# Prompt delta rule: projections as three passes of high and low parts, tokens split once, outputs kept in memory, the turns of k and v moved

## The reference

```python
proj = h @ w_in                                   # q_a, k_a, v_a, z_a: 8 heads x 128 columns each
q, k, v = silu(causal_conv(concat(q_a, k_a, v_a)))  # 4 taps
q = l2norm(q) * DK ** -0.5;  k = l2norm(k)
...
# chunked form of S_t = a_t S_{t-1} (I - b_t k_t k_t^T) + b_t k_t v_t^T,  o_t = S_t^T q_t
L = A + eye;  sol = triangular_solve(L, [v * beta, kb * exp(gc)])
def chunk_step(S, ...):
    v_new = u_n - w_n @ S
    o_n = q_n @ S + qk_n @ v_new
    S = S * ge + k_n.T @ v_new
...
o_a = rmsnorm(o_a, gdn_norm) * silu(z_a)
merged = sigmoid(gate_a) * (o_a @ w_br_gdn) + sigmoid(gate_b) * (o_b @ w_br_swa)
```

## Time and profile before

| | us |
|---|---|
| median of 3 runs | 3023.04 (3020.31 to 3026.46) |
| the profiled execution | 3019.03 |
| its span in the profile | 3017.4 |
| TensorE busy | 2488.4 (82%), 12055 records |
| VectorE busy | 1534.6 (51%) |
| ScalarE busy | 1060.1 (35%) |
| GpSimd busy | 390.5 (13%) |
| mean granted TensorE clock | 0.895 |

### The profile page before, as it was taken

One profiled execution on the slowest core, in us unless ns is written; L12 is line 12 of the kernel. 1 busy time (PEld: TensorE's weight loads), 2 busy tenths in 40 slices (PEclk: granted clock), 3 DMA queues, 4 the chain that ended last, 5 costly groups with the idle time before them and its releaser, 6 DMA issues. The chain is left out here.

```text
span 3017.4 us, 34539 instructions
## 1 busy us (share of the span) xinstructions
PE 2488.4 (82%) x12055; PEld 1842.5 (61%) x12056; DVE 1534.6 (51%) x2016; ACT 1060.1 (35%) x1517; POOL 390.5 (13%) x434
## 2 busy tenths in 40 slices
PE   4789999999995756789986989888937999999940
PEld 2367666776674633644445989883426888888720
DVE  2155455545544312124446464633346888888805
ACT  3123323322331100023333333321206777777702
POOL 1012012101201120012222000000022111111003
PEclk7899999999997757589997999999968999999965
DMA  7411111111101023031105544444246999999625
GB/s 287 169 38 37 37 30 52 36 37 30 52 5 49 19 83 129 1 84 42 42 1 195 148 125 145 127 141 151 78 176 261 401 405 406 405 403 403 258 104 188
DMA packets 313391, 436.14 MB, mean 145 GB/s; under 512 B 56354, under 2 KB 254514, under 8 KB 293539
## 3 DMA queue, kind: packets, MB, share of 16 engines
q1 hardware_dynamic: 289164, 370.93, 34.9%
q0 software_dynamic: 11168, 39.12, 3.5%
q10 hardware_dynamic: 13000, 25.30, 2.2%
HBM read 384.40 MB, written 52.94 MB: 145 GB/s over the span
## 5 line engine op out<-in xcount | busy, mean ns | idle before, releaser
L2417 DVE TENSOR_TENSOR ex_w_r<-ex_w,ex_wh 128x2048 fp32r<-128x2048 f32 x192 | 433.2, 2284 | 59.7 <-ACT ex_wh L2359 59.6
L2359 ACT ACTIVATE ex_wh<-ex_w 128x2048 fp32r<-128x2048 f32 x192 | 367.7, 1917 | 130.6 <-PEq L2066 43.0
L828 PE MATMUL gd_ps<-hT,gd_w 128*128 128x352 f32 x768 | 252.3, 483 | 8.1 <-DMA gd_w<-in_w_in_dram 7.4
L1779 PE MATMUL mg_psum<-mg_xl,mg_wh 128*128 128x352 f32 x768 | 251.4, 327 | 0.0
L828 PEld LDWEIGHTS gd_ps<-hT,gd_w 128*128 128x128 f32 x768 | 151.6, 202 | 91.0 <-issue 13.8
L1839 DVE TENSOR_TENSOR mg_w_r<-mg_w,mg_wh 128x1024 fp32r<-128x1024 f32 x96 | 133.9, 1399 | 118.8 <-ACT mg_wh L1792 118.4
L1792 ACT ACTIVATE mg_wh<-mg_w 128x1024 fp32r<-128x1024 f32 x96 | 101.3, 1056 | 183.2 <-DVE mg_out L1866 120.1
L1951 PE MATMUL op_mix<-op_w,op_mT 128*128 128x512 f32 x288 | 130.6, 613 | 25.0 <-DMA op_w<-in_w_out_dram 25.0
L1779 PEld LDWEIGHTS mg_psum<-mg_xl,mg_wh 128*128 128x128 f32 x768 | 147.7, 192 | 0.0
L1779 PE MATMUL mg_psum<-hT_r,mg_wh 128*128 128x352 f32 x384 | 126.2, 329 | 18.4 <-DVE mg_w_r L1839 18.4
L1475 PE MATMUL wp_proj_psum<-hT,wp_wq 128*128 128x512 f32 x256 | 116.2, 608 | 14.0 <-DMA wp_wk<-in_w_in_dram 8.8
(11 more groups left out here) (576 smaller groups left out, 5195.0 us busy)
## 6 DMA issues: line engine op xcount, KB each, us to landing
ex_w<-in_w_gate_dram SPq DMA_DIRECT2D x64, 1024.0 KB, 8.0
ex_w<-in_w_up_dram SPq DMA_DIRECT2D x64, 1024.0 KB, 7.4
ex_w<-in_w_down_dram SPq DMA_DIRECT2D x64, 1024.0 KB, 8.6
ada_w<-in_w_ada_dram SPq DMA_DIRECT2D x24, 1024.0 KB, 16.0
mg_w<-in_w_in_dram SPq DMA_DIRECT2D x48, 512.0 KB, 3.5
gd_w<-in_w_in_dram SPq DMA_DIRECT2D x32, 512.0 KB, 4.2
expert_out_scratch<-ex_y ACTq DMA_DIRECT2D x32, 512.0 KB, 7.7
mg_w<-in_w_br_gdn_dram SPq DMA_DIRECT2D x24, 512.0 KB, 3.9
```

What stands on the lines that cost most here:

```text
L828: last = nc.tensor.matmul(dst, w[t][:, n, :], c.hT[:, n, at], start=(n == 0), stop=(n == KD - 1))
L1779: last = nc.tensor.matmul(pm[b][q][:, 0:R], a, x, start=(m == 0 and v == 0), stop=(m == KD - 1 and v == 2))
L2359: nc.scalar.activation(wh[at][:], wl[b][u][:], ACT.Copy).then_inc(w_high, 1)
L2417: nc.vector.tensor_tensor(wl_r[b][u][:], wl[b][u][:], wh[at][:].bitcast(F32), ALU.subtract).then_inc(w_low, 1)
```

## The change

- All projections of `delta_prompt` become three passes of fp32r: `wh` (high part of the weight, two buffers for four weights), `w_r` (its low part, in place of the weight), `hh` and `hl` (the two parts of the tokens; the low part lies in place of `hT`).
- For each weight and head, ACT casts the high part (`high`) and VectorE subtracts it (`low`). Both are put at fixed places in the streams.
- Before the first head the tokens are split in eight steps on ACT and VectorE, with the q projection of head 0 following step by step. Behind the last head GpSimd adds the halves up into `hT` again.
- The outputs go to `qd` and from there to memory (`c.oa_s`); `conv_outputs` loads them back into `c.oaT`, which is now allocated behind `delta_prompt`. `nwT` shares a buffer with `k2`.
- TensorE does the first third of the next q ahead of the turn of k, and the turn of v within level 4 instead of ahead of it.

```diff
@@ sync: body, behind the store of the state
+                    for g in range(2):
+                        sp.wait_ge(o_done, i * 2 + g + 1)
+                        sp.dma_start(c.oa_s[bass.ds(i, 1), :, g * C4:(g + 1) * C4].rearrange("a p t -> (a p) t"), qd[g][:]).then_inc(oa_stored, 16)
...
                 sp.wait_ge(stored, 16 * H)
+                sp.wait_ge(oa_stored, 32 * H)
@@ gpsimd: behind the heads
+                for n in range(KD):
+                    pool.wait_ge(v_proj, 3 * H)
+                    nc.gpsimd.tensor_tensor(c.hT[:, n, :], hl[:, n, :].bitcast(F32), hh[:, n, :].bitcast(F32), ALU.add).then_inc(joined, 1)
@@ scalar
+                def high(t, j):
+                    act.wait_ge(w_loaded[t], j * 16 + 16)
...
+                    nc.scalar.activation(half_of(t)[:], w[t][:], ACT.Copy).then_inc(w_high, 1)
@@ scalar: body
                         nc.scalar.activation(DT[g][:], E[g][:], ACT.Exp).then_inc(dt, 1)
+                    if nxt:
+                        high(0, i + 1)
                     for t in range(2):
...
                     evac(2, 2, i)
+                    if nxt:
+                        high(1, i + 1)
+                        evac(0, 0, i + 1)
                     for g in range(2):
                         act.wait_ge(turned, i * 2 + g + 1)
                         nc.scalar.activation(kt[g][:], X[g][0][:], ACT.Copy).then_inc(kts, 1)
-                    if nxt:
-                        evac(0, 0, i + 1)
...
+                        high(3, i + 1)
...
+                    if nxt:
+                        high(2, i + 1)
                     for g in range(2):
                         act.wait_ge(wt, i * 2 + g + 1)
                         nc.scalar.activation(nwT[g][:], pp[g][:], ACT.Copy, scale=-1.0).then_inc(nw, 1)
@@ scalar: before the heads
+                high(0, 0)
+                for n in range(KD):
+                    nc.scalar.activation(hh[:, n, :], c.hT[:, n, :], ACT.Copy).then_inc(h_high, 1)
+                high(1, 0)
@@ vector
+                def low(t, j):
+                    dve.wait_ge(w_high, split_count(t, j))
+                    nc.vector.tensor_tensor(w_r[t][:], w[t][:], half_of(t)[:].bitcast(F32), ALU.subtract).then_inc(w_low, 1)
@@ vector: body; low(0) stands before the norms, low(3) behind level 5, low(2) in the last chunk
                     dve.wait_ge(normed, i * 4 + 4)
+                    dve.wait_ge(oa_stored, i * 32)
...
                     conv(2, i, 0, CONV)
+                    if nxt:
+                        low(1, i + 1)
                     solve(i)
...
-                        nc.vector.scalar_tensor_tensor(c.oaT[:, bass.ds(i, 1), at].rearrange("p a t -> p (a t)"), E[g][:], 0.5, DT[g][:], ALU.mult, ALU.mult).then_inc(o_done, 1)
+                        nc.vector.scalar_tensor_tensor(qd[g][:], E[g][:], 0.5, DT[g][:], ALU.mult, ALU.mult).then_inc(o_done, 1)
@@ vector: before the heads
+                low(0, 0)
+                for n in range(KD):
+                    dve.wait_ge(h_high, n + 1)
+                    nc.vector.tensor_tensor(hl[:, n, :], c.hT[:, n, :], hh[:, n, :].bitcast(F32), ALU.subtract).then_inc(h_low, 1)
+                low(1, 0)
...
-                for t in range(2):
-                    conv(t, 0, 0, CONV)
+                low(3, 0)
+                conv(0, 0, 0, CONV)
+                low(2, 0)
+                conv(1, 0, 0, CONV)
@@ tensor
+                def passes(t, n, at):
+                    return ((half_of(t)[:, n, :], hh[:, n, at]), (half_of(t)[:, n, :], hl[:, n, at]), (w_r[t][:, n, :], hh[:, n, at]))
...
-                        last = nc.tensor.matmul(dst, w[t][:, n, :], c.hT[:, n, at], start=(n == 0), stop=(n == KD - 1))
+                        for v, (a, b) in enumerate(passes(t, n, at)):
+                            last = nc.tensor.matmul(dst, a, b, start=(n == 0 and v == 0), stop=(n == KD - 1 and v == 2))
@@ tensor: body
+                    if nxt:
+                        pe.wait_ge(v_evac, i * 3 + 3)
+                        for half in range(2):
+                            project(0, 0, half, i + 1)
                     for g in range(2):
                         pe.wait_ge(ats, i * 8 + g * 4 + 4)
                         turn(X[g][0], y[1], g).then_inc(turned, 1)
                     if nxt:
-                        pe.wait_ge(v_evac, i * 3 + 3)
-                        for u in range(3):
+                        for m in range(1, 4):
                             for half in range(2):
-                                project(0, u, half, i + 1)
-                    pe.wait_ge(v_silu, i + 1)
-                    pe.wait_ge(capped, i * 8 + 8)
-                    for g in range(2):
-                        turn(pp[g], y[2], g).then_inc(vturned, 1)
...
+                                project(m // 3, m % 3, half, i + 1)
@@ tensor: levels, between the two products of level 4
-                        if nxt and l > 4:
+                        if l == 4:
+                            pe.wait_ge(v_silu, i + 1)
+                            pe.wait_ge(capped, i * 8 + 8)
+                            for g in range(2):
+                                turn(pp[g], y[2], g).then_inc(vturned, 1)
+                        elif nxt:
                             project(1, l - 4, 0, i + 1)
@@ conv_outputs, sync
                 sp.dma_start(c.wkv[:], kmajor(w_in[0])[:, :, CKB:CKB + 2 * KVH * DH]).then_inc(c.kv_loaded, 16)
+                sp.dma_start(c.oaT[:, :, 0:T], c.oa_s.rearrange("h p t -> p h t")).then_inc(oa_loaded, 16)
...
                 sp.wait_ge(stored, 32)
+                sp.wait_ge(oa_loaded, 16)
```

More of the change, by code:

```diff
@@ L444, in delta_prompt @@
         k = Kit(nc, ctx)
-        w = [k.sb(f"gd_w{t}", [P, KD, P]) for t in range(4)]
+        w, w_r = zip(*(k.sb_reused(f"gd_w{t}", [P, KD, P]) for t in range(4)))
+        wh = [k.sb(f"gd_wh{n}", [P, KD, P], F32R) for n in range(2)]
+        hh, hl = k.sb("gd_hh", [P, KD, TA], F32R), c.hT_r
         pre = k.sb("gd_pre", [P, 3, CONV - 1 + T])
@@ L456, in delta_prompt @@
         grp = lambda n: [k.sb(f"gd_{n}{g}", [P, C4]) for g in range(2)]
-        E, DT, qd, qkm, AT, Y, YT, T1, k2, kdt, vt, nwT = (grp(n) for n in (
-            "E", "DT", "qd", "qkm", "AT", "Y", "YT", "T1", "k2", "kdt", "vt", "nwT"))
+        E, DT, qd, qkm, AT, Y, YT, T1, k2, kdt, vt = (grp(n) for n in (
+            "E", "DT", "qd", "qkm", "AT", "Y", "YT", "T1", "k2", "kdt", "vt"))
+        nwT = k2
         am = [[k.sb(f"gd_am{g}{b}", [P, C4]) for b in range(2)] for g in range(2)]
@@ L469, in delta_prompt @@
         gn_loaded = sem("gd_gn_loaded")
+        w_high, w_low, h_high, h_low, oa_stored, joined = (sem("gd_" + n) for n in ("w_high", "w_low", "h_high", "h_low", "oa_stored", "h_joined"))
+        RANK = (0, 1, 3, 2)
         halo, staged, qk_taps, qk_proj, qk_evac, v_proj, v_evac, z_proj, z_evac = (sem("gd_" + n) for n in (
@@ L593, in evac @@
                     src = pp[u % 2] if t == 3 else (pps, pv, pps)[u]
+                    if t == 0 and u == 2 and isinstance(j, int) and j == 0:
+                        src = pp[0]
                     if t == 3 and u == 0:
@@ L777, in body @@
                             nc.vector.tensor_copy(YT[g][:], X[g][1][:]).then_inc(yts, 1)
-                        if nxt and l == 4:
-                            conv(0, i + 1, 2, CONV)
+                        if nxt:
+                            if l == 4:
+                                conv(0, i + 1, 2, CONV)
+                            else:
+                                low(3, i + 1)
                     for g in range(2):
@@ L796, in body @@
                                 silu_qk(1, i + 1)
+                            if ch == CONV + 3:
+                                low(2, i + 1)
                     for g in range(2):
@@ L840, in z_unit @@
                         pe.wait_ge(z_evac, j * 3 + 1)
-                    last = nc.tensor.matmul(pp[u % 2][:, 0:C3], w[3][:, k_, :], c.hT[:, k_, u * C3:(u + 1) * C3], start=(k_ == 0), stop=(k_ == KD - 1))
+                    for v, (a, b) in enumerate(passes(3, k_, slice(u * C3, (u + 1) * C3))):
+                        last = nc.tensor.matmul(pp[u % 2][:, 0:C3], a, b, start=(k_ == 0 and v == 0), stop=(k_ == KD - 1 and v == 2))
                     if k_ == KD - 1:
@@ L971, in body @@
                         nc.tensor.matmul(X[g][1][:], c.ones[:], T1[g][:], start=True, stop=True).then_inc(o_sum, 1)
-                for t in (0, 1, 3):
+                pe.wait_ge(w_low, 1)
+                for n in range(KD):
+                    pe.wait_ge(h_low, n + 1)
+                    for u in range(3):
+                        for v, (a, b) in enumerate(passes(0, n, slice(u * C3, (u + 1) * C3))):
+                            last = nc.tensor.matmul((pps, pv, pp[0])[u][:, 0:C3], a, b, start=(n == 0 and v == 0), stop=(n == KD - 1 and v == 2))
+                        if n == KD - 1:
+                            last.then_inc(qk_proj, 1)
```

(1 more changed line is left out.)

37 lines of the change are left out of this document (25 added, 12 removed).

## The result

The changed kernel takes 3031.89 us (median of 20 runs, 3026.16 to 3037.59) against 3023.94 for the kernel before in the same comparison: a ratio of 1.0024, 95% interval 1.0015 to 1.0032. The prediction said 3033, slower. TensorE is busy for less time, 2419.7 us where it was 2488.4, and the kernel takes longer.

What follows compares the result with a forecast made beforehand. A chain over ScalarE, TensorE, VectorE and DMA up to level 4, not TensorE, bounds each head; +2 - 16 + 14.6 + 2.5 + 7 = +10.1 us on the median of 3023.04 gives 3033, range 3012 to 3050.

Steps and rivals of the forecast that it cites:

- start: Before the first head: subtractions and casts ahead of convolutions and tanh, z's last unit waiting longer; +2 us, 0 to +4.
- seven periods: Seven heads with a next one: period 100.55 us against a mean of 102.81, 2.26 less each; -16 us together.
- last head: Last head: three v units give 3.0 us, turn of v costs 2.0, GpSimd's additions cost 15.6; together +14.6.
- joins: Last head: GpSimd's eight additions of token halves each let one VectorE solve step pass; +15.6 us, 0 if steps slip between.
- last output store: Behind the heads: the block's end waits for the last output store and its issue; +2.5 us, 0 to 5.
- reload in `conv_outputs`: Behind the heads: 4 MB of outputs loaded back behind wkv make the next stage start 7 us later, 4 to 11.
- low(1): Between convolution and solve on VectorE: subtraction for k's weights lies on the chain to level 4; +1.2 us, 0 to 2.2.
- Rival (A): Heads: TensorE sets the period, so its saved 84 us come out; change of -58 us, 2965 us; chance 7%.
- The scores: Ahead of level 4: the scores start 2.1 us earlier, after the waiting cast of q's weights; bounds 3.0 and 0.
- Rival (C): Ahead of the scores: q's weights land 2 us or more later than forecast, scores gain nothing; 3048 us; chance 16%.
- The half clock and the turn of v: From level 4 on: first products at 1.2 GHz after idle time, v's transposition behind them; +4.1 us per head.
- Rival (B): Last head: GpSimd's additions of the token halves cost nothing; -5.5 us, 3017.5 us; chance 17%.

Runs made afterwards that it cites:

- the old order: The changed kernel with the turns of k and v and q's first third back where they were, projections in three passes: 3018.02 us, ratio 0.9973.
- the two runs on the joins: Changed kernel with GpSimd's last-head additions waiting for the solve's end: 3016.49 us, ratio 0.9969; changed kernel with each addition cut in two: 3033.82 us, one run.
- the order alone: The kernel before with only the turns of k and v and q's first third moved, projections still full fp32: 3042.71 us, ratio 1.0055.

## Why the prediction was right

Its forecast case came, by its own terms, measured from the start of the last decay sums and the stages around them:

| term | forecast | measured |
|---|---|---|
| start | +2 | -0.1 (158.82 against 158.92; see below) |
| seven periods | -16 | -18.1 (701.84 against 719.90) |
| last head | +14.6 | +15.8: 14.5 up to level 4 (joins +17.1, the rest -2.6), 1.3 from there to the outputs |
| last output store | +2.5 | +2.3 |
| reload in `conv_outputs` | +7 | +6.1 |
| sum | +10.1 | +6.1 |

- **The bound.** The two parts of a head, 50.35 and 50.2 us, came out at 50.39 and 49.81. That the chain sets the first is shown by the runs with low(1) and with the solve moved. Rival (A) falls: over heads 1 to 6 TensorE's busy time fell by 9.9 us a head (96.5 to 86.6), of which 7.3 became idle time (6.3 to 13.6) and 2.6 shortened the head. The prediction read the floor's distance, 2.6 us, from head 1, whose first part of 53.84 us was an unusual one before; in the other heads with a next one it was 52.64 to 52.68. The sum used 51.25 and the mean period and is not touched by this.
- **The scores**, 2.1 us earlier, came 2.3 earlier. The waiting cast did delay the roots by 2.2 us, but only 0.3 of it counted: TensorE itself was not ready for the scores much sooner. Rival (C) did not come: in heads 1 to 6 q's load, issued behind the stores, landed in 3.6 to 3.8 us (4.2 taken), and ScalarE waited 0.9 to 1.2 us for it (1.3 taken).
- **low(1)**, 1.2, took 2.06 beside GpSimd, inside its bound; of these about 1.4 reached level 4 (50.39 - 51.25 + 2.3).
- **The half clock and the turn of v**, +4.1, were sized too high with three passes: the two orders differ by 3.0 us from level 4 on (by 3.8 in full fp32). The products took 2.07 us as forecast, but the turn took 1.04 to 1.92 us in heads 1 to 6, 1.43 on average, where the forecast had 1.97. What TensorE's shorter projections give back behind level 4 was sized too high as well: 3.1 us (49.95 against 46.84, both in the old order), where the forecast had 2.0 + 2.1 - 0.3 = 3.8. The two misses partly cancel, so the match of the second part is in part luck.
- **The joins**, 15.6, took 17.1: a join lasted 2.37 us beside the solve instead of 1.95, and its step was as long. Rival (B) falls with the two runs on the joins.
- **The start**, +2, came out at -0.1 in this pair of profiles, but what ran ahead of it took a different time in the two: the first load of projection weights goes out at 104.90 us in the changed kernel and at 105.73 before. From that load to the first decay sums it took 53.2 us before, and 53.2 in the run with the order alone, which has the old start; in the changed kernel and the eleven experiments with its start it took 53.9 to 55.3, 54.6 by the median. So the start costs some 1.4 us: the sign was right.
- **The seven periods** vary too: three experiments that leave them as they are took 702.3 to 704.2 us, so the 701.84 of this profile is at the short end.

The forecast stood 10 us above the median of before; 8 were measured, of which this pair of profiles shows 6.1 up to the sample stage. The other 2 are within the spread of the start, of the periods and of the stages behind. That 3033 and 3031.89 lie so close is in part luck, since the terms of the sum were off by 0.2 to 2.1 us, some up and some down.

## What to carry to other kernels

Ask of a saving on the busiest engine which wait ends last in each stretch: here 9.9 us a head saved on TensorE became 7.3 us of idle time and 2.6 us of time, and moving one convolution on VectorE off the chain gained 35 us, where the whole change lost 8. Work that is put on an idle GpSimd is not free while VectorE runs a chain of short steps that read SBUF alone; put it beside steps that read an operand from PSUM. When work leaves the time ahead of a wait, look at what runs at the half clock behind it.

## What the runs showed of the hardware

Beside the solve one VectorE step passed for each GpSimd instruction: 0.2 us steps became 2.33, 1.22 or 0.97 us beside additions of 2.37, 1.26 and products of 1.04 us. Even a copy of three elements per partition, with a single operand in SBUF, took 2.37 us beside the joins and 0.16 without. The half clock behind idle time took 1.3 us a head where a pair of runs shows it by itself, and the new order, which brought it about, had gained only 0.8 ahead of level 4. The same eight products took 2.07 us after 11.56 us of idle time and 1.05 after k's third, although that third itself had begun at the half clock (0.29 us a product, 0.16 at its end).
